# The first three units of a convolution mixer: weights in blocks of 128 channels, and a second chunk computed before the norm's factor

## What is computed

```python
def rmsnorm(x, g):
    y = x * rsqrt(mean(x * x, axis=-1) + EPS)
    return y * g

h = rmsnorm(x, pre_norm_g[0])
a, g, z = split(h @ a_w_in, 3)       # 1024 x 3072
c = a * sigmoid(g)                   # then a causal depthwise convolution of 31 taps over c
out = (silu(layernorm(conv(c))) * silu(z)) @ a_w_out
```

## Time and profile before

| | us |
|---|---|
| median of 3 runs | 2219.28 |
| lowest, highest | 2219.01, 2219.78 |
| profiled execution, its span | 2219.2 |
| busy in the span: TensorE | 2207.4 |
| VectorE | 1596.2 |
| ScalarE | 967.3 |
| GpSimd | 356.6 |

### The profile page before, as it was taken

One profiled execution on the slowest core, in us unless ns is written; L12 is line 12 of the kernel. 1 busy time (PEld: TensorE's weight loads), 2 busy tenths in 40 slices (PEclk: granted clock), 3 DMA queues, 4 the chain that ended last, 5 costly groups with the idle time before them and its releaser, 6 DMA issues.

```text
span 2219.2 us, 29963 instructions
## 1 busy us (share of the span) xinstructions
PE 2207.4 (99%) x11815; PEld 1943.6 (88%) x11815; DVE 1596.2 (72%) x1988; ACT 967.3 (44%) x1454; POOL 356.6 (16%) x517
## 2 busy tenths in 40 slices
PE   9999999999999999999999999999999999999998
PEld 7888899999888888888888888888889999998887
DVE  6889999998798988999986227852296666667321
ACT  6443333333453225665665125542236656656110
POOL 1211111111221111121110101210112121120000
PEclk9999999999999999999999999999999999999999
DMA  8556566564444313333345426352213333236321
GB/s 295 194 152 152 148 181 185 154 166 129 172 172 167 107 70 113 109 102 125 107 128 217 151 101 217 139 180 88 85 63 93 104 98 107 87 101 248 135 95 38
DMA packets 135292, 303.75 MB, mean 137 GB/s; under 512 B 18160, under 2 KB 54768, under 8 KB 133616
## 3 DMA queue, kind: packets, MB, share of 16 engines
q1 hardware_dynamic: 106192, 203.27, 27.3%
q0 software_dynamic: 28960, 98.57, 15.5%
HBM read 223.40 MB, written 78.75 MB: 136 GB/s over the span
## 4 chain that ended last, share of the span: by engine, by line
PE 94%; DVE 4%; DMA 1%; issue 0%; ACT 0%; SPq 0%; POOL 0%; ACTq 0%; POOLq 0%
PE PS L2340 29%; PE PS L2342 29%; PE PS L2341 29%; PE PS L2591 2%; DVE acc L1720 2%; DVE over L1747 1%; PE PS L2347 1%; PE PS L2346 1%; PE PS L2455 1%; PE PS L2433 1%; DMA raw<-wa_in_in 0%; DMA rawb<-wb_out_in 0%; DMA st<-s_scratch 0%; DVE cs L1765 0%; PE PS L2442 0%
## 5 line engine op out<-in xcount | busy, mean ns | idle before, releaser
L1720 DVE SCALAR_TENSOR_TENSOR acc<-cp,cw,acc 128x513 f32<-128x513 f32 (+3 forms) x464 | 367.5, 792 | 14.3
L2340 PE MATMUL PS<-HAh,Wh 128*128 128x512 f32 (+2 forms) x960 | 341.1, 355 | 3.4 <-DVE HAl L1663 1.8
L2341 PE MATMUL PS<-HAl,Wh 128*128 128x512 f32 (+2 forms) x960 | 339.2, 353 | 0.0
L2342 PE MATMUL PS<-HAh,Wl 128*128 128x512 f32 (+2 forms) x960 | 339.1, 353 | 0.0
L2340 PE MATMUL PS<-Vh,HBh 128*128 128x512 f32 x512 | 199.6, 390 | 0.0
L2342 PE MATMUL PS<-Vh,HBl 128*128 128x512 f32 x512 | 199.2, 389 | 0.0
L2341 PE MATMUL PS<-Vl,HBh 128*128 128x512 f32 x512 | 199.2, 389 | 0.0
L2340 PEld LDWEIGHTS PS<-HAh,Wh 128*128 128x128 f32 x960 | 180.7, 188 | 19.8 <-DVE Wl L1658 3.5
L1747 DVE SCALAR_TENSOR_TENSOR over<-pair,cg,over 128x512 f32<-128x512 f32 (+1 forms) x240 | 189.9, 791 | 7.4
L2340 PE MATMUL PS<-Wbh,s7h 128*128 128x512 f32 x500 | 195.1, 390 | 0.0
L2342 PE MATMUL PS<-Wbh,s7l 128*128 128x512 f32 x500 | 194.6, 389 | 0.0
(11 more groups left out here) (254 smaller groups left out, 5226.1 us busy)
## 6 DMA issues: line engine op xcount, KB each, us to landing
raw<-wa_in_in SPq DMA_DIRECT2D x48, 512.0 KB, 4.5
Wl<-wa_in_in POOLq DMA_DIRECT2D x39, 512.0 KB, 5.6
rawv<-wb_v_in SPq DMA_DIRECT2D x64, 256.0 KB, 4.6
QWr<-wb_uz_in SPq DMA_DIRECT2D x64, 256.0 KB, 2.6
v_scratch<-vb POOLq DMA_DIRECT2D x64, 256.0 KB, 2.6
vt<-v_scratch SPq DMA_DIRECT2D x32, 512.0 KB, 3.9
s_scratch<-m POOLq DMA_DIRECT2D x32, 512.0 KB, 4.0
rawb<-wb_out_in SPq DMA_DIRECT2D x28, 512.0 KB, 8.1
```

Of the source, the lines that this page charges most:

```text
L1720: return nc.vector.scalar_tensor_tensor(out=out, in0=src, scalar=w, in1=first, op0=ALU.mult, op1=ALU.add)
L2340: nc.tensor.matmul(out, wh, xh, start=start, stop=False, skip_group_check=seeded)
L2341: nc.tensor.matmul(out, wh, xl, start=False, stop=False, skip_group_check=seeded)
L2342: return nc.tensor.matmul(out, wl, xh, start=False, stop=stop, skip_group_check=seeded)
```

## The change

Four things are changed, all in the first 70 us.

1. The weights of the first three units (KEEP = 3) come from a second copy in memory, `wa_first`, laid out by blocks of 128 input channels: block k holds 128 x 128 weights of each of the three units, 192 KB. ScalarE and VectorE split a block for all three units at once (`first_weight_high`, `first_weight_low`). On each partition the block lands in three pieces of 128 numbers. The buffers are where units 0 to 2 had theirs.
2. TensorE takes chunk 0 of the three units block by block: the three matmuls with high parts, then the three with HAl, then the three with Wl.
3. Chunk 1 of all three units also uses tokens without the factor. They are loaded to a buffer xg[1], and the factor is put on with `first_factor`, `first_sigmoid`, `first_gate` and `first_silu` for both chunks. The tokens with the factor for chunk 1 are made afterwards, for units from 3 on.
4. Tiles are squared in their natural order, 0 to 7, and (3,0), (4,0) come ahead of (3,1), (4,1).

```diff
-AHEAD_A = {(3, 1): 5, (4, 0): 6}
+SECOND_ROWS = [(n, k) for k in range(KH) for n in range(3)] + [(n, k) for n in range(3) for k in range(KH, KD)]
+AHEAD_A = {(4, 0): 5, (4, 1): 6}
...
-        a_order = list(FIRST) + [(3, 1), (4, 1), (3, 0), (4, 0)]
+        a_order = list(FIRST) + [(3, 0), (4, 0), (3, 1), (4, 1)]
...
+            def first_load(k):
+                sp.dma_start(firstr[:, :, 1, k * P:(k + 1) * P], wa_first[k, :, :, :]).then_inc(n1_ldk[k], 16)
...
+            x_row(0, 0)
+            sp.dma_start(par[:, :], chan_par).then_inc(ld_filters, 16)
+            first_load(0)
+            for k in range(1, KD):
+                x_row(k, 0)
+                first_load(k)
             sp.dma_start(con[:, :], consts).then_inc(ld_con, 16)
+            x_load(0)
+            x_load(1)
+            x_row(0, 1)
+            x_load(2)
+            x_row(1, 1)
+            x_load(3)
+            for k in range(2, KD):
+                x_row(k, 1)
+            a_load(3)
             for t in range(4, 8):
                 x_load(t)
...
+            def first_weight_high(k):
+                act.wait_ge(n1_ldk[k], 32)
+                ks = slice(k * P, (k + 1) * P)
+                nc.scalar.activation(firsth[:, :, 0, ks], firstr[:, :, 1, ks], ACT.Copy).then_inc(a_hi, 1)
...
             for k in range(KD):
+                first_weight_high(k)
+                first_high(k, 0)
+            n1_square(0)
+            n1_square(1)
+            first_high(0, 1)
+            n1_square(2)
+            first_high(1, 1)
+            n1_square(3)
+            for k in range(2, KD):
+                first_high(k, 1)
             n1_factors(0)
+            first_sigmoid(0)
+            for k in range(3):
+                n1_high(k, 0)
+                if k > 0:
+                    n1_square(k + 3)
+            first_silu(0)
+            for k in range(3, KD):
+                n1_high(k, 0)
+                if k < 5:
+                    n1_square(k + 3)
+            n1_factors(1)
             a_high(3)
+            first_sigmoid(1)
+            n1_square(8)
+            n1_square(9)
+            first_silu(1)
+            n1_high(0, 1)
+            a_high(4)
+            for k in range(1, KD):
+                n1_high(k, 1)
+                if k >= 4:
+                    n1_square(k + 6)
...
             def a_first_chunks():
+                for k in range(KD):
+                    pe.wait_ge(a_hi, k + 1)
+                    pe.wait_ge(n1_hi, k + 1)
+                    for n in range(KEEP):
+                        nc.tensor.matmul(PS[:, n, :], first_weights(n, k)[0], HAh[0][:, k, 0:CW], start=k == 0, stop=False)
...
+                for t in range(4):
+                    n1_spread(t)
+
+            def a_second_chunks():
+
+                for n, k in SECOND_ROWS:
+                    pe.wait_ge(n1_lo, KD + k + 1)
+                    last = a_row(n, 1, k)
                     if k == KD - 1:
                         last.then_inc(a_mm, 1)
+                    if (n, k) == (0, KD - 1):
+                        for t in range(4, 8):
                             n1_spread(t)
```

More of the change, by code:

```diff
@@ L231, in build @@
         zc = r("zc", [P, WIDTH[1]])
-        xg = Region(r2_at, c_at)("xg", [P, KD, CW])
+        xg = [Region(r2_at + KD * CW * 4 * i, c_at)(f"xg{i}", [P, KD, CW]) for i in range(2)]
         xq = [Region(r2_at + KD * WIDTH[1] * 4 + 4 * D * i, c_at)(f"xq{i}", [P, D]) for i in range(8)]
@@ L1160, in _ @@
             pool.wait_ge(c_neg, 2)
-            for t in X_ORDER[0:8]:
+            for t in range(8):
                 n1_rsqrt(t)
@@ L1616, in _, with first_sigmoid @@
-            n1_factors(0)
-            a_high(3)
-            act.wait_ge(a_norm, 1)
-            nc.scalar.activation(cs[:, 0:CW], cs[:, 0:CW], ACT.Sigmoid).then_inc(a_sig, 1)
-            for k in range(2):
-                n1_high(k, 0)
-            a_gate(0, 1)
-            n1_high(2, 0)
-            a_high(4)
-            n1_high(3, 0)
+            def first_sigmoid(c):
+                half = cs[:, c * CW:(c + 1) * CW]
+                act.wait_ge(a_norm, 3 * c + 1)
+                nc.scalar.activation(half, half, ACT.Sigmoid).then_inc(a_sig, 1)
@@ L2279, in _ @@
             nc.vector.memset(vmv[:, :, :], 0.0).then_inc(c_pad, 1)
-            a_low(0)
-            first_low(0)
-            first_low(1)
-            first_low(2)
-            a_low(1)
-            first_low(3)
-            a_low(2)
-            for k in range(4, KD):
-                first_low(k)
+            for k in range(KD):
+                first_low(k, 0)
+                first_weight_low(k)
             for i, n in ((0, HIST), (CONV_W[0] + HIST, 2), (CONV_W[1] + HIST, 2)):
                 nc.vector.memset(cp[:, i:i + n], 0.0).then_inc(c_pad, 1)
+            for k in range(KD):
+                first_low(k, 1)
+            first_factor(0, 0)
+            n1_scale(0, 0)
+            n1_scale(1, 0)
+            first_gate(0)
+            n1_low(0, 0)
+            n1_scale(2, 0)
+            dve.wait_ge(a_norm, 2)
+            a_product(1, 0)
+            n1_low(1, 0)
+            first_factor(2, 0)
+            for k in range(3, KD):
+                n1_scale(k, 0)
+                n1_low(k - 1, 0)
+            n1_low(KD - 1, 0)
+            a_low(3)
+            first_factor(0, 1)
+            first_gate(1)
+            dve.wait_ge(a_norm, 5)
+            a_product(1, 1)
+            first_factor(2, 1)
             n1_scale(0, 1)
-            for k in range(1, KD):
+            n1_scale(1, 1)
+            n1_low(0, 1)
+            a_low(4)
+            for k in range(2, KD):
                 n1_scale(k, 1)
@@ L2367, in a_row @@
                 p, s, h = a_pos[n, c], n % 3, n // UNITS_A
-                return three(PS[:, p % A_BANKS, 0:w], Wh[s][:, k, :], Wl[s][:, k, :], HAh[h][:, k, c0:c0 + w],
+                wh, wl = first_weights(n, k) if n < KEEP else (Wh[s][:, k, :], Wl[s][:, k, :])
+                return three(PS[:, p % A_BANKS, 0:w], wh, wl, HAh[h][:, k, c0:c0 + w],
                              HAl[h][:, k, c0:c0 + w], k == 0, k == KD - 1)
             def a_first_chunks():
-                for i, (n, k) in enumerate(FIRST_ROWS):
-                    if k == 0:
-                        pe.wait_ge(a_lo, n + 1)
-                    pe.wait_ge(n1_lo, k + 1)
-                    last = a_row(n, 0, k)
+                for k in range(KD):
+                    pe.wait_ge(a_hi, k + 1)
+                    pe.wait_ge(n1_hi, k + 1)
+                    for n in range(KEEP):
+                        nc.tensor.matmul(PS[:, n, :], first_weights(n, k)[0], HAh[0][:, k, 0:CW], start=k == 0, stop=False)
+                    pe.wait_ge(n1_lo, k + 1)
+                    for n in range(KEEP):
+                        nc.tensor.matmul(PS[:, n, :], first_weights(n, k)[0], HAl[0][:, k, 0:CW], start=False, stop=False)
+                    pe.wait_ge(a_lo, k + 1)
+                    for n in range(KEEP):
+                        last = nc.tensor.matmul(PS[:, n, :], first_weights(n, k)[1], HAh[0][:, k, 0:CW], start=False,
+                                                stop=k == KD - 1)
+                        if k == KD - 1:
+                            last.then_inc(a_mm, 1)
```

230 lines of the change are left out of this document (87 added, 143 removed).

## The result

| | us | (5,0) starts |
|---|---|---|
| before, median of 5 runs (lowest to highest) | 2219.36 (2219.01 to 2219.78) | 68.15 |
| changed kernel, median of 5 runs | 2226.66 (2225.76 to 2228.63) | 72.66 |
| ratio, 95% interval | 1.0035 (1.0024 to 1.0047) | |

The changed kernel is slower by 7.3 us, 0.33%. The forecast was 2220.4, with a range of 2217.2 to 2223.2: wrong in size, and on the wrong side of the 0.2% bound. The profiled execution of the changed kernel took 2225.76 us, its span is 2224.0.

The account below looks back on a forecast made before the run. TensorE was taken as a queue of matmuls that never runs dry, so (5,0), the first chunk behind all reordered ones, shows the change: 2219.2 - 5.7 + 3.6 + 1.5 + 1.2 + 0.6 = 2220.4 us, range 2217.2 to 2223.2.

Parts of the forecast that it names:

- the base: Starting number of the sum: the profiled span of 2219.2 us, treated as one with the median of 2219.28.
- the packets: First units' weights landing in 512 B pieces in the saturated queue: +0.6 us on (5,0), between 0 and +1.3.
- part 5: Unit 5's low weights behind four convolution steps that need c copied: TensorE waits 1.2 us, (5,0) starts at 68.8.
- Part 1: Start, weights by blocks of 128 channels: TensorE starts at 6.5 without gaps, second chunks at 23.3 instead of 29.05, lead 5.7 us.
- Part 2: Second chunks without the factor: raw tokens are cast by 26 us, TensorE reaches them at 31.5, no wait.
- Part 3: ScalarE's chain to tile 7's square, ending at 37.4: TensorE waits 3.9 us from 34.2, the stage takes 3.6 us more.
- rival (d): 512 B pieces cost twice the time in the saturated queue, 3.9 us more: 2223.7 us, slower beyond measure; 6%.
- rival c: Clock falls after a wait: absorbed after the 3.9 us wait, in full ahead of (5,0), giving 2222.0 us; 10%.
- Part 4: Unit 4's weights behind ScalarE's chain: low weights end at 50.9, TensorE at 49.4 waits 1.5 us, lead 0.6 us.
- (a): The start's lead is kept, ScalarE's chain is not the bound and TensorE meets no wait: 2213.5 us; 5%.
- (b): Only the last wait goes because c is back earlier, (5,0) at 67.6: 2218.6 us, or 2219.2; 17%.
- (e): Block 0 lands late and TensorE starts at 7.9 as before: still 2220.4 us, counted with the forecast, 62% together.

Follow-up runs that it names:

- pairs: Changed kernel with the first units' weights loaded two blocks at a time, 1 KB pieces in four transfers instead of 512 B in eight: 2224.54 us, ratio 1.0023.
- the transposes late: Changed kernel with the transposes of tiles 4 to 7 behind all second chunks instead of behind unit 0's: 2226.67 us, ratio 1.0033.

## Why the prediction was wrong

**The steps that failed** are three: the base (span and median taken as one number), the size of the term for the packets (+0.6), and the time of GpSimd in part 5 (0.9 us from tile 10's square to the store of c). The chain that the prediction followed and the order of its stations held, but for a wait of 1.68 us at the first transposes that it had put at nothing.

**The whole miss** is 6.3 us (2226.66 against 2220.4). It splits into 3.3 us of landmark (72.66 against 68.15 + 1.2 = 69.35), 0.3 us behind the landmark, 0.9 us by which the changed kernel's median lies above its profiled execution, and 1.8 us between span and time. The 3.3 us are 1.5 of packets (2.1 for 0.6), 1.6 of GpSimd and 0.6 of other lateness of tile 10's square, less 0.4 gained between the store and (5,0).

**The base** ("the two are treated as one"). Wrong by 1.8 us. That span and median agreed to 0.1 us was chance: the execution was slow by about as much as time and span differ. The lead of 5.7 us was counted against that slow execution too. Against the one in which the clock stays up, the second chunks of the changed kernel begin 1.6 us earlier; of what is missing, 1.8 is the base (27.27 for 29.05) and 2.4 the changed kernel's own lateness (25.67 for 23.3, next paragraph).

**Part 1, the start.** The first real matmul starts before 7 us, without a gap, at full clock: right. Then TensorE waits 1.68 us at the transposes of tiles 0 to 3, which I had put at no wait: the squares of these tiles stand behind the slow weights, and the last ends at 24.6, 22.1 in my chain. 25.67 instead of 23.3. All four traces with 512 B pieces have this wait (1.40 to 2.47 us), of the five of the changed kernel with larger pieces only one (1.50).

**Part 2.** No wait for the raw second-chunk tokens: right.

**Part 3, ScalarE's chain.** The mechanism was right and so were its terms but one. First square 17.98 (15.9 foreseen), square 7 ends at 39.8 (37.4), the last transpose runs at 40.85 (38.4). The wait ahead of it is 3.5 us in two pieces (3.9). The term that was wrong is the **packets**: +0.6 foreseen, +2.1 in the first square. The experiments with larger pieces give 1.7 to 2.0 us of square in single traces, 1.4 in the mean of nine, and 1.8 to 2.1 us of time. The row I took as nearest, v's reload in 512 B pieces, came from a stretch where the queue isn't full, as I had noted, and I still put the value on its side. The Trainium skill ("DMA: Bandwidth & Descriptors", Specifications) gives 512 B as the least piece for full rate. The traces disagree: 303 to 345 GB/s in the full queue, against 372 to 398 for pieces of 1 KB and 1.5 KB. The first square came 2.1 us late, more than my bound (a third more time, +1.3) and less than rival (d) (twice the time, +3.9); what larger pieces give back in the mean is near that bound.

**The clock** (rival c). In the profiled execution it fell after the waits for the roots, as that rival said, and the twelve matmuls at half clock cost 2.4 us. I had called this absorbed, because unit 4's weights come late anyway. That is nearly what happened: TensorE reached (4,0) after the weights (ready at 53.5), so the foreseen wait of 1.5 us was filled by it, and VectorE got the last chunk of the group late (idle 1.48 us), which put silu 0.3 us later. The same cost has an open end elsewhere. In the kernel whose blocks land in one piece, TensorE waited 2.85 us ahead of (5,0), and its first matmul there shows the clock down:

```profile
71.41 0.75 PE L2362 MATMUL PS<-HAh,Wh 128*128 128x512 f32 x1 [2.85 <-DVE Wl L1672]
```

That execution took 2152.2 us behind (5,0); with pairs, after a wait of 2.44 us and the clock up (0.50 us for the matmul), 2150.5. I read the spread of the changed kernel's executions, and why removing the last wait gave 3.8 us for 2.2 to 2.6 us of landmark, as this: behind a wait there the clock sometimes falls. It is argued from two traces; the executions at 2228 us were not profiled. Nor does the length of a wait decide by itself: with the transposes late, the clock was still at 1.00 behind a wait of 2.89 us (45.18) and fell soon after one of 2.27 us (53.20).

**Part 4.** Unit 4's high weights end at 52.3, 49.6 foreseen: late by the packets, with the order of stations right.

**Part 5, the last wait.** Place and mechanism right, 1.26 us (1.2 foreseen), as one side of it was late as well as the other. The copy of c was stored at 60.88 (56.6 foreseen): 2.7 us by tile 10's square (57.28 against 54.6) and 1.6 us by GpSimd, for which I had taken the durations of the kernel before, where other VectorE steps stood beside it. Its addition ran from 58.49 to 59.91, beside two VectorE steps that both read two operands from SBUF (58.49 to 59.83), and in all eight variants of the changed kernel it took 1.42 us again, beside the same steps. In the kernel before, the step beside it takes its factor from PSUM (`HAr<-xg,par,PS`, at 53.84) and the addition took 0.22. The Trainium skill ("GPSIMD Engine Reference", Specifications) says that GpSimd shares its SBUF interfaces with VectorE and contends with instructions of two SBUF inputs. The rows agree. No experiment isolated it, and one row goes against a simple rule: at 57.90 of the kernel before, an addition that began together with such a step took 0.22 us, and only the root behind it was long, 0.85.

**The rivals.** (a) and (b) did not come. (e), that the start fails, did not either. (d), slower beyond measure, had the right cause and 6%: it needed pieces at half rate. The pieces did not reach that; the base error and GpSimd made up for it and more, so its outcome would have been right by luck. I had listed terms of one sign each as separate cases; they add.

## What to carry to other kernels

Before counting what can be saved in a stretch, find out whether the profiled execution is a typical one: compare its own time, not its span, with the median. A transfer in a full queue is not to be priced by a row from a quiet stretch, and neither is a small GpSimd operation by one that had other VectorE steps beside it. When a step moves from where its engine waited for another into a place where it has to run at its own cost, count the empty gap it leaves: the squares cost little where they stood, and moving them ahead cost 5.3 us.

## What the runs showed of the hardware

- In the changed kernel, from 7 to 15.5 us and with the DMA engines' share at 0.96 to 1.10, pieces of 512 B moved at 303 and 345 GB/s, pieces of 1 KB at 372 and 385 and of 1536 B at 385 and 398. Four transfers of the 1 KB kind and eight of the 1536 B kind put the first square at 16.00 and 16.28, 512 B pieces at 17.98.
- A GpSimd addition on 128 x 1 numbers took 0.22 us in most places, and 1.42 us in all nine traces of the changed kernel and its variants, where it began together with the first of two VectorE steps of two SBUF inputs, `HAr<-xg,par,rnc` and `HAl<-HAr,HAh`. That these steps are the cause is not isolated.
- The granted clock of the kernel before fell at 12 us in two traces (waits of 1.48 and 1.83 us just before) and not in a third, with one more input that is never read (1.28 us). (5,0) came 1.7 us earlier there, the end 0.8 to 1.2 us.
- The time of an execution was 1.74 to 1.86 us above its span, in every kernel.
